# A hybrid decoder layer on one core: the opening of the input projection is rearranged (norm weight spread by TensorE, a fourth row buffer, two weights opened together)

## What is computed

```python
def rmsnorm(x, g):
    xf = x.astype(jnp.float32)
    y = xf * lax.rsqrt(jnp.mean(xf * xf, axis=-1, keepdims=True) + EPS)
    return (y * g.astype(jnp.float32)).astype(x.dtype)

h = rmsnorm(x, w['pre_g'])          # (1056 tokens, 1024)
u = h @ w['w_in']                   # (1056, 3584): q k v z of attention, x o z of the mLSTM
qa, ka, va, za, xb, ob, zb = jnp.split(u, SPLITS, axis=-1)
```

## Time and profile before

| what | value |
|---|---|
| median of 3 runs | 992.28 us |
| the three runs | 991.8, 992.28, 998.51 us |
| the profiled execution | 997.07 us |
| its span in the profile | 995.4 us |
| PE busy | 930.8 us (94%), 6963 matmuls |
| DVE busy | 490.2 us (49%) |
| ACT busy | 389.4 us (39%) |
| POOL busy | 108.6 us (11%) |

### The profile page before, as it was taken

How to read it: one execution, slowest core, us unless ns; L and a number is a source line. 1 busy time by engine, 2 the same in 40 slices (tenths; PEclk the granted TensorE clock), 3 DMA queues, 4 the chain that set the end, 5 groups by cost and what they waited for, 6 DMA issues and landing times.

```text
span 995.4 us, 18461 instructions
## 1 busy us (share of the span) xinstructions
PE 930.8 (94%) x6963; PEld 749.5 (75%) x6963; DVE 490.2 (49%) x1079; ACT 389.4 (39%) x832; POOL 108.6 (11%) x233
## 2 busy tenths in 40 slices
PE   3999989999999999998799999998869999999996
PEld 3999989999888888887566667765547786577774
DVE  4634844555474345444475655455464443533222
ACT  5533253433334643333544544454453222421211
POOL 1300000000000000002000023331011000000000
PEclk9989999999999999999999999999999999999998
DMA  6362215222332222223977779967984422203221
GB/s 216 105 172 65 65 50 142 65 64 65 101 106 65 85 64 66 82 65 117 344 247 216 233 256 337 345 220 239 313 283 176 180 85 69 64 18 131 74 90 42
DMA packets 115265, 142.36 MB, mean 143 GB/s; under 512 B 9623, under 2 KB 75799, under 8 KB 115178
## 3 DMA queue, kind: packets, MB, share of 16 engines
q1 hardware_dynamic: 109418, 122.31, 38.4%
q0 software_dynamic: 5760, 18.88, 5.6%
HBM read 125.34 MB, written 15.41 MB: 141 GB/s over the span
## 4 chain that ended last, share of the span: by engine, by line
PE 83%; ACT 4%; DMA 4%; DVE 3%; SPq 3%; issue 2%; POOL 1%; POOLq 0%; ACTq 0%; DVEq 0%
PE ps L1944 72%; PE ps L1947 10%; DMA Vr<-in_cache_v 1%; SPq L579 1%; DMA Kr<-in_cache_k 1%; DMA xrow<-in_x_prompt 1%; PE ps L1939 1%; ACT U L922 1%; SPq L575 1%; DVE pp L1758 0%; ACT wh L938 0%; ACT junk L1214 0%; ACT pp L1136 0%; POOL small L734 0%; DVE kTs L1723 0%
## 5 line engine op out<-in xcount | busy, mean ns | idle before, releaser
L1944 PE MATMUL ps<-hhi,whi 128*128 128x272 f32 (+1 forms) x672 | 229.1, 341 | 1.1 <-DVE hlo L1279 1.1
L1944 PE MATMUL ps<-hhi,wlo 128*128 128x272 f32 (+1 forms) x672 | 219.8, 327 | 0.0
L1944 PE MATMUL ps<-hlo,whi 128*128 128x272 f32 (+1 forms) x672 | 219.2, 326 | 0.0
L1944 PE MATMUL ps<-wh,r 128*128 128x512 f32 (+1 forms) x544 | 154.8, 401 | 0.1
L1944 PEld LDWEIGHTS ps<-hhi,whi 128*128 128x128 f32 x672 | 129.5, 193 | 13.8 <-issue 3.7
L1944 PEld LDWEIGHTS ps<-hlo,whi 128*128 128x128 f32 x672 | 129.5, 193 | 9.9 <-issue 1.9
L1944 PEld LDWEIGHTS ps<-hhi,wlo 128*128 128x128 f32 x672 | 129.2, 192 | 9.2
L1944 PEld LDWEIGHTS ps<-wh,r 128*128 128x128 f32 (+1 forms) x544 | 99.1, 185 | 26.1 <-issue 1.0
L1295 DVE TENSOR_TENSOR wlo<-wst,whi 128x1024 fp32r<-128x1024 f32 x56 | 69.2, 1236 | 80.4 <-ACT whi L897 80.4
L1723 DVE COPY kTs<-ps 128x512 f32<-128x512 f32 x64 | 44.1, 689 | 66.6 <-PE ps L1947 66.5
L1947 PEld LDWEIGHTS ps<-ident,Kr 128*128 128x128 f32 x512 | 56.3, 141 | 25.5 <-issue 22.0
(11 more groups left out here) (351 smaller groups left out, 1372.0 us busy)
## 6 DMA issues: line engine op xcount, KB each, us to landing
Kr<-in_cache_k SPq DMA_DIRECT2D x128, 256.0 KB, 4.2
wst<-in_w_in SPq DMA_DIRECT2D x56, 512.0 KB, 3.9
Vr<-in_cache_v POOLq DMA_DIRECT2D x72, 256.0 KB, 4.8
Vr<-in_cache_v SPq DMA_DIRECT2D x56, 256.0 KB, 4.0
out_y_prompt<-rows SPq DMA_DIRECT2D x16, 512.0 KB, 2.9
xrow<-in_x_prompt SPq DMA_DIRECT2D x8, 512.0 KB, 5.1
wout<-in_w_out SPq DMA_DIRECT2D x8, 512.0 KB, 5.5
rows<-in_x_prompt SPq DMA_DIRECT2D x8, 512.0 KB, 4.4
```

The costliest lines, as they stand in the source:

```text
L1944: return nc.tensor.matmul(out, lhsT, rhs, start=start, stop=stop, **more)
```

## The change

Seven edits, nearly all of them in the head:

- `gpre` is read as one row of 4 KB into one partition. PE multiplies it by a row of ones into PSUM banks 2 and 3 (two matmuls of 512 columns, f32), and DVE copies that to all 128 partitions before its first `scale_x`.
- `xrow` has four buffers; SP asks for tile o once tile o - 4 is scaled.
- SP's queue: weight 1 comes right after row tile 3, weight 2 after tile 5, and the eleven parameter DMAs stand behind row tile 6.
- The two halves of `U0` are 256 and 288 columns (`COLS`), where both were 272.
- The first four pieces are, in this order: first half of weight 0, first half of weight 1, second half of weight 0, second half of weight 1 (`OPENING`). The first needs row tiles 0 and 1, the third row tiles 0 to 4.
- PE does piece 0 after turn 2, and one more piece than before has been done at each later step: pieces 0 to 5 stand between the turns, 6 before the parameters' transpose, 7 before the state rows' transposes, 8 right behind them, 9 behind `weights_T`, 10 behind `folded`, and so on, until a later `fill(11)` becomes `fill(10)`. The fills of ACT and DVE move along. Row tile 2 is turned into banks 0 and 1.
- The semaphore `kvtok_ready`, for which nothing waited, goes.

```diff
-PIECE = FIRST // 2
+COLS = (slice(0, 2 * P), slice(2 * P, FIRST))
-WEIGHTS_DONE = [2 * w + 2 if w < NT else NT + w + 1 for w in range(WEIGHTS)]
+OPENING = [(0, 0), (1, 0), (0, 1), (1, 1)]
+WEIGHTS_DONE = [3, 4] + [2 * w + 2 if w < NT else NT + w + 1 for w in range(2, WEIGHTS)]
+def piece_at(p):
+    return OPENING[p] if p < len(OPENING) else divmod(p, 2)
+def head_bank(o):
+    return 0 if o == 2 else 4 + 2 * ((o if o < 2 else o - 1) % 2)
-        xrow.append(place("xrow2", [P, D], offset=u0_base))
+        xrow += [place(f"xrow{2 + n}", [P, D], offset=u0_base + n * D * 4) for n in range(2)]
         def bank_of(event):
-            return event % 4
+            return (event + 2) % 4
@@ SP
-                if o >= 3:
-                    sp.wait_ge(s["h_ready"], o - 2)
+                if o >= 4:
+                    sp.wait_ge(s["h_ready"], o - 3)
             load_x(0)
-            sp.dma_start(gpre, io["norm_pre_g"][0:1, :].broadcast_to([P, D])).then_inc(s["gpre_in"], 16)
+            sp.dma_start(gpre[0:1, :], io["norm_pre_g"][0:1, :]).then_inc(s["gpre_in"], 16)
             load_x(1)
             load_w(0)
             load_x(2)
+            load_x(3)
+            load_w(1)
+            load_x(4)
+            load_x(5)
+            load_w(2)
+            load_x(6)
...
-            for o in range(3, 9):
-                load_x(o)
-                if o in (4, 6):
-                    load_w(o // 2 - 1)
+            load_x(7)
+            load_x(8)
             load_heads(0)
@@ ACT
-            for o in range(3):
-                square_x(o)
+            square_x(0)
+            square_x(1)
+            split(0)
+            square_x(2)
             store_hi(0)
-            split(0)
+            square_x(3)
             store_hi(1)
-            square_x(3)
             store_hi(2)
-            square_x(4)
-            store_hi(3)
-            for o in range(4, 9):
+            fill()
+            for o in range(3, 9):
                 if o < 8:
                     square_x(o + 1)
-                fill()
                 store_hi(o)
-            fill()
+                if o < 8:
+                    fill()
...
-            fill()
+            fill(2)
             act.wait_ge(*done["hist_ready"])
@@ DVE
-            dve.wait_ge(s["gpre_in"], 16)
+            dve.wait_ge(*done["gpre_spread"])
+            nc.vector.tensor_copy(gpre, ps[:, 2:4, :].rearrange("p a b -> p (a b)")).then_inc(*signal["gpre_stored"])
+            dve.wait_ge(*done["gpre_stored"])
-            for o in range(3):
-                scale_x(o)
+            scale_x(0)
+            scale_x(1)
+            rest(0)
+            scale_x(2)
             store_lo(0)
-            rest(0)
             store_lo(1)
             scale_x(3)
             store_lo(2)
-            scale_x(4)
-            store_lo(3)
-            for o in range(4, 9):
+            fill()
+            for o in range(3, 9):
                 if o < 8:
                     scale_x(o + 1)
-                fill()
                 store_lo(o)
+                if o < 8:
+                    fill()
@@ PE
+            pe.wait_ge(s["gpre_in"], 16)
+            for c in range(2):
+                last = nc.tensor.matmul(ps[:, 2 + c, :], ones[0:1, :], gpre[0:1, c * 512:(c + 1) * 512], start=True, stop=True)
+            last.then_inc(*signal["gpre_spread"])
             def turn_h(o):
-                if o >= 2:
-                    pe.wait_ge(s["hlo_ready"], o - 1)
+                if o >= 3:
+                    pe.wait_ge(s["hlo_ready"], o - 2 if o < 5 else o - 1)
             def piece(p):
-                w, part = p // 2, p % 2
+                w, part = piece_at(p)
-                if p < 2:
-                    pe.wait_ge(s["hlo_ready"], (3, 5)[p])
+                if p < len(OPENING):
+                    pe.wait_ge(s["hlo_ready"], (2, 5)[part])
-            for o in range(4):
+            for o in range(3):
                 turn_h(o)
-            for o in range(4, 9):
-                if o == 4:
-                    fill()
-                    turn_h(o)
-                else:
-                    fill()
-                    turn_h(o)
+            for o in range(3, 9):
+                fill()
+                turn_h(o)
             fill()
```

More of the change, by code:

```diff
@@ L430, in program @@
         s = {n: sem(n) for n in names}
-        once = {"pe": """vecT_ready hist_ready nT_ready weights_T folded s_q_proj s_k_proj s_v_proj s_gates s_kvtok s_sqk s_GT
+        once = {"pe": """gpre_spread vecT_ready hist_ready nT_ready weights_T folded s_q_proj s_k_proj s_v_proj s_gates s_kvtok s_sqk s_GT
             s_AB s_inter s_intra s_obT s_nrow s_hT state_ready krow_ready vrow_ready xbrow_ready last3_ready as_T_ready as_T2
@@ L443, in program @@
                 signal[name], done[name] = (steps_done, 1), (steps_done, n + 1)
-        x_in = [sem(f"x_in{n}") for n in range(3)]
+        x_in = [sem(f"x_in{n}") for n in range(4)]
         w_in = [sem(f"w_in{n}") for n in range(3)]
@@ L886, in square_x @@
                 t, n = HEAD[o], XT[HEAD[o]][1]
-                act.wait_ge(x_in[o % 3], 16 * (o // 3 + 1))
+                act.wait_ge(x_in[o % 4], 16 * (o // 4 + 1))
                 if o >= 1:
                     act.wait_ge(s["sumsq_ready"], o)
-                nc.scalar.activation(square[0:n, :], xrow[o % 3][0:n, :], ACT.Square, scale=D ** -0.5,
+                nc.scalar.activation(square[0:n, :], xrow[o % 4][0:n, :], ACT.Square, scale=D ** -0.5,
                                      accum_out=sumsq[0:n, t:t + 1]).then_inc(s["sumsq_ready"], 1)
@@ L910, in evict @@
                 if e < 2 * NT:
-                    tile, c = ORDER[e // 2], e % 2
-                    nc.scalar.activation(U0[:, tile, c * PIECE:(c + 1) * PIECE], ps[:, bank_of(e), 0:PIECE], ACT.Copy
-                                         ).then_inc(s["u_stored"], 1)
+                    w, c = piece_at(e)
+                    out = U0[:, ORDER[w], COLS[c]]
+                    nc.scalar.activation(out, ps[:, bank_of(e), 0:out.shape[1]], ACT.Copy).then_inc(s["u_stored"], 1)
                 else:
@@ L1061, in _ @@
                 chunk(i)
-            fill(12)
+            fill(11)
             act.wait_ge(s["conv_step"], CONV_SECOND)
@@ L1288, in scale_x @@
                     dve.wait_ge(s["hT_ready"], o - 1)
[L1289 removed]
+                nc.vector.scalar_tensor_tensor(out=hrow[0:n, o % 2, :], in0=xrow[o % 4][0:n, :],
                                                scalar=rstd[0:n, t:t + 1], in1=gpre[0:n, :],
@@ L1665, in _ @@
             finish(H - 1)
-            fill(3)
+            fill(2)
             dve.wait_ge(s["piece_done"], 2 * NT)
@@ L1962, in piece @@
                 if p < 2 * NT:
-                    out, ks, hi, lo = ps[:, bank_of(e), 0:PIECE], range(KC), hhi[0], hlo[0]
-                    cols = slice(part * PIECE, (part + 1) * PIECE)
+                    cols = COLS[part]
+                    out, ks, hi, lo = ps[:, bank_of(e), 0:cols.stop - cols.start], range(KC), hhi[0], hlo[0]
                 else:
@@ L2125, in chunk @@
                 for h in range(H):
-                    last = turn(ps[:, 4, h * P:(h + 1) * P], x[h])
-                last.then_inc(s["kvtok_ready"], 1)
+                    turn(ps[:, 4, h * P:(h + 1) * P], x[h])
                 if i == 0:
@@ L2187, in _ @@
             finish(H - 1)
-            fill(11)
+            fill(10)
             for i in range(H, CH):
```

13 lines of the change are left out of this document (6 added, 7 removed).

## The result

The changed kernel takes 1001.87 us in the median of 15 runs (998.2 to 1007.01). The kernel before, timed beside it, takes 994.32 us in the median of 15 (991.27 to 998.51). The ratio is 1.0068, with a 95% interval of 1.0053 to 1.0084: some 6.8 us slower (5.3 to 8.4), where 7.5 were predicted. That is less than the 1% that the prediction gave as what one measurement can tell, but over this many runs it lies clear of zero. The profiled execution took 1002.61 us with a span of 1001.0, against 997.07 and 995.4 before, so the two profiles stand 5.6 apart.

What follows compares the result with a forecast made beforehand. PE, 83% of the chain, was taken to bound the kernel. Terms 0.8 + 1.8 + 2.4 + 1.6 + 0.9 gave +7.5 us, 999.8 on the median 992.28; forecast's own range 997 to 1002 (40%), overall range 989 to 1004.5.

Steps and rivals of the forecast that it cites:

- T8: End of the head's last turn: about 45.6 (43.2 to 46.6) against 44.99, with pieces 0 to 5 done; head gain 2.5 us.
- moved piece waits for weight 4: Behind the state rows' transposes: piece 8 now comes next and PE waits 4.9 us for weight 4's rest; net +0.8 us.
- clock behind it: Piece 8, behind the wait for weight 4: it runs at the lower clock; +1.8 us (0 to 2.6).
- tenth piece ahead of the convolution: DVE makes weight 6's rest before the sample's convolution; PE resumes at F + 6.9, F being the small products' end; +2.4 us.
- clock behind that: Behind the convolution's idle stretch of nearly 4 us: slow clock for the products and the piece; +1.6 us (0 to 2.6).
- `s_hn`: At piece 24: DVE makes weight 13's rest ahead of `s_hn`, PE at 128.6 instead of 127.74; +0.9 us (0 to 1.2).
- columns and parity: 256 and 288 columns cost nothing (upper end 4.3 us); pieces of changed parity in the chunks 0 (-1 to +1).
- Piece 0 runs at the lower level: First piece in the head, starting at 18.2: 24 x 256 columns at 1.2 GHz take 5.1 us.
- The spread: Start of the head: row at 5.1, two matmuls 3.6 us, copy 1.3, so first `scale_x` at 10.2 instead of 7.23.
- the head's gain passing through: Rival, 15%: producers are ready, so PE's two new waits don't occur; -2.5 us and 0.9 for `s_hn`, about 990.5.
- Only one of the two waits: Rival, 25%: weight 4 is late, but the convolution isn't, or the clock doesn't fall behind it; 995.8 us.
- The clock stays low longer: Rival, 17%: both slow stretches at 2.6 and T8 a microsecond later, or the 288 columns dear; 1003 to 1007 us.

Runs made afterwards that it cites:

- run 2: The changed kernel with weights 4 and 5 asked for right behind weight 3, ahead of SP's parameter waits: 1000.5 us, ratio 1.0047 to before.
- run 3: The changed kernel with DVE's rest of weight 6 moved behind the sample's convolution: 999.73 us, ratio 1.0036 to before.
- run 4: The changed kernel with the edits of run 2 and run 3, and `s_hn` ahead of the rest of weight 13: 994.27 us, ratio 0.9975 to before.
- run 1: The changed kernel with its new head, but the piece behind the last turn put back on PE, ACT and DVE: 998.85 us, ratio 1.0023 to before.
- run 7: The kernel of run 4 without SyncE's waits for `vec_ready` and `lam_ready` ahead of the state rows: 990.87 us, ratio 0.9938 to before.
- run 5: The changed kernel with the norm weight again as a broadcast transfer of 512 KB, without the spread: ratio 1.0086 to before.
- run 6: The changed kernel with pieces of 272 and 272 columns, the first pieces waiting for the third tile's low half: ratio 1.0138 to before.
- run 11: The kernel of run 7 with the moved piece put back and weight 5 asked for behind the state rows: 997.93 us, ratio 0.9989 to before.
- run 8: The kernel before with weights 4 and 5 asked for behind weight 3 and no parameter waits of SyncE: ratio 1.0002 to before.
- run 9: The kernel before with weight 4 behind weight 3, no parameter waits ahead of the state rows, weight 5 behind them: 996.4 us, ratio 0.9979 to before.
- run 10: The kernel of run 5 with two matmuls of the spread's shape, which nothing reads, ahead of the first turn: ratio 1.0064 to before.

## Why the prediction was right

Term by term, on the profiled executions:

| term | predicted | measured |
|---|---|---|
| T8, with six pieces done | 45.6 | 45.43 |
| moved piece waits for weight 4 | +0.8 | 58.44 + 1.23 - 59.19 = +0.5 |
| clock behind it (piece 8, 4.33 for 2.85) | +1.8 | +1.5 |
| tenth piece ahead of the convolution (F + 6.8 for F + 4.5) | +2.4 | +2.3 |
| clock behind that (9.27 for 6.20) | +1.6 (0 to 2.6) | **+3.1** |
| `s_hn` (wait 3.44 for 2.56) | +0.9 | +0.9 |
| columns and parity, to 306.67 | 0 (-1 to +1) | **-1.7** |
| sum | +7.5 | +6.6 |

The sum agrees with the +6.53 read at 306.67. That it comes so near the predicted 7.5 is partly luck: the two terms that were wrong, 1.5 us too little for the clock and 1.7 us that came back later, nearly cancel. So is the absolute time: 999.8 was 7.5 us above a before of 992.28, and over 15 runs before is at 994.32 and the change at 1001.87, at the edge of the forecast's 997 to 1002.

The mechanism was right: the two waits of PE, on the rest of weight 4 and on the convolution's SiLU, are where and what they were said to be. Runs 2 to 4 confirm the terms in the profiles: asking for weight 4 early took away the wait and the slow clock of piece 8, putting the convolution first took away most of the lateness of `s_q_proj` and all of the slow clock behind it, `s_hn` ahead of its rest its 0.9.

*The head's gain.* Right at T8, but partly by luck. The step "Piece 0 runs at the lower level" failed: it ran at the full clock, in 2.9 us instead of 5.1, and piece 2 started at 27.14 instead of 29.3. The gain was given back at once: behind its wait of 1.75 us piece 2 took 4.79 us, where a piece of 288 columns at the full clock takes 3.27. Neither is always so. In seven profiles of this head piece 0 ran at the full clock five times and took 4.4 us in runs 3 and 4; piece 2 ran slow only in the change's and in run 4's. So T8 was 43.6 to 43.9 in runs 1, 2 and 7, and 46.9 in run 4, and the head's gain at T8 is 1 to 4.4 us from one execution to the next, 2.6 in the one profiled.

*The spread.* Costed right (PE 3.75, first `scale_x` at 10.09 for 10.2), but run 5 shows no gain of the head that comes from it. The row was there at 5.05, 0.3 behind tile 0 (ACT squares that one from 4.76); the lower bound of 3.4 wasn't reached. By the rule that the prediction weighed, of the Trainium skill's page "DMA: Bandwidth & Descriptors", section "Queues, rings and completion order" (each engine takes its descriptors in ring order, which puts a one-row transfer behind its engine's share of the tile ahead), the row was to come at 5.1. The trace agrees with that time.

*Columns.* As columns, 256 and 288 for 272 twice cost nothing, as I said. But the sum started piece 0 when the low halves of tiles 0 and 1 stood, and that they are enough is the columns' doing; the edit that I listed among those at nothing carried the head's gain. Run 6 gives it a price: 5 to 7 us.

*Clock behind the convolution.* The term of +1.6 was mis-sized: it measured 3.1, beyond its bound of 2.6. I had priced it as one piece's loss; but there are two units of work behind that wait, small products and a piece, and the clock stayed low through much of both (4.28 us for 2.97, and 4.97 for 3.17). PE's idle time there, which I put at 3.9, was only 2.18, because piece 10 ran slow and filled it: the low clock was free in piece 10 and dear behind it.

*Parity.* Wrong by more than its bound: with the piece gone from the late stage 0.59 comes back beyond the piece itself, 0.12 in each of three chunks, and 0.7 between the turn of `kbT` and the first chunk. Run 11 shows the same from the other side (34.21 against 34.07, and 3.68 for a piece of 3.05). This says where the 1.7 us come back; which of the fills on ACT and DVE gives them was not tried.

Of the rivals, the head's gain passing through (990.5, that is 1.8 below before) is what the kernel becomes when its two waits are taken away (run 4, 2.5 below before, good to 2): the rival named the right condition, and the change didn't meet it. "Only one of the two waits" (995.8) is excluded by the waits of 4.5 and 2.2 in one profile, and by its ratio too (995.8 / 992.28 is 1.0035, under the interval). "The clock stays low longer" was right about the stretch behind the convolution only.

Open: how much run 2's edit alone is worth; what in the order of the turns decides when the clock first rises; and why the clock falls behind a short wait in one execution and not in the next.

## What to carry to other kernels

When one unit of work is moved forward, look up when each of its inputs comes at its new place, on every queue, before counting what it saves: here it met one weight 4.5 us too early, and an unchanged number of fills on DVE put an optional rest ahead of a critical convolution. Move the requests with the work: the same move that cost 4.5 us by the times (run 1) was worth 5 (run 11) once the requests of weight 4 and of the state rows and two fills on DVE had followed it. And a wait on a queue is a wait for all that stands behind it: taking away one of SyncE's waits gave nothing while a request for a busy buffer stood in the same place (runs 8 and 9).

## What the runs showed of the hardware

- An idle stretch is priced by what follows it. Ahead of `s_q_proj` PE waited 2.0 to 2.4 us in the change and in runs 2, 5, 6 and 10, and each time its next stretch of small products and a piece took 9.1 to 9.3 us at a mean clock of 0.62 or 0.63. After 0.90 us it took 6.3 at 1.00 in runs 3 and 4 and 7.76 at 0.78 in run 7. In the head (waits of 1.0 to 1.8 us) and at piece 8 (1.4 us, runs 2 and 4) the clock fell in some executions of the same order and not in others, at 1.4 to 1.5 us a time.
- The clock also falls with no idle stretch. In the kernel before PE ran without a gap from 53.31, and at 67.1 the matmuls of piece 9 became slow (4.48 us for the piece, mean clock 0.65). The piece at this place, behind the small products, was slow in 9 of the 13 profiles and at the full clock in runs 3, 4, 7 and 8. What decides this no run shows.
- In the head the change's clock was up behind three turns run as one block of 5.49 us, and stayed up over the 1.07 us of idle time ahead of piece 0; in runs 3 and 4 it was up at the third turn and piece 0 was slow after 1.4 us. In run 6 it was up at the third turn and down at the next piece, after 3.69 us of idle time. With gaps of 1.1 to 1.4 us between the turns it rose only 2.4 us (run 5) and 2.7 us (run 10) into piece 0, so 3.78 us of matmuls put ahead of them in run 10 brought nothing.
- Two f32 matmuls of one row by 512 columns stand in the profile as four instructions and take 3.75 us; the turns right behind them run at half speed, so I take this for the lower clock too. One with 128 rows took 1.10 us at the full clock, so two would be 4.4 at half of it, by estimate. One row in place of 128 saves little.
